# Encoder layer with dilated attention on one core: scores and value products both on 64x64 tiles of the array

## The chip, the core and the metric

The kernel runs on one NeuronCore of a Trainium2 chip. Its engines have names in the profile: PE is TensorE (matmuls; PEld are its weight loads), DVE is VectorE, ACT is ScalarE, POOL is GpSimd, and SP issues most DMAs. The metric is the device time of one execution in microseconds (us), as the median of several runs. A lower number is better.

## What is computed

Two independent sequences (1024 tokens, width 1024, float32) pass through one encoder layer. Cut to what matters here:

```python
h = rmsnorm(x, norm_mix)
z = h @ w_in                                   # pool channels, then q, k, v of 12 heads of 64
a = pool_mixer(z[..., :512], pool_maps, pool_scale) @ w_up_pool
b = attention_branch(z[..., 512:]) @ w_up_attn
gates = sigmoid(h @ w_gate + b_gate)
x = x + (g_a * a + g_b * b) @ w_out
h = rmsnorm(x, norm_ffn)
x = x + (silu(h @ w_ffn_gate) * (h @ w_ffn_up)) @ w_ffn_down
return rmsnorm(x, norm_final)
```

`attention_branch` has three groups of four heads with dilations 1, 4 and 16. Each query sees the keys of a window around it (`softmax(q k^T / 8) v`), and the three groups are merged by a softmax over their log-sum-exp values. `pool_mixer` takes window means of four channel groups and multiplies each group with a 128x128 map.

## The kernel before

**The large products.** All large matrix products are done in three float32r matmuls each (high x high, low x high, high x low part, lines 1080 to 1082) and by a seven-product scheme: "product m" (`pair_product`) is twelve matmuls over 512 columns on the full 128x128 array. In the front part there are 133 such products per sequence (`FRONT`), and their sums go through banks 0 to 3 of PSUM, which has eight banks.

**The attention** is woven into these products by a fixed schedule. A *unit* is 128 queries of one pair of heads, a *duo* is two units, and there are 24 duos per sequence: duos 0 to 7 are group 0 (a query tile sees up to 256 keys that lie in two tiles of values, so the value products of its two units are separate), 8 to 15 group 1 (both units of a duo share their keys), 16 to 23 group 2 (128 keys each). From product `ATT0` on, duo `d` takes these steps:

- `scores(d)`: per unit and head h one plain float32 matmul, with the 64 rows of the head as contraction and 128 queries as columns, thus on a 64x128 tile of the array, into bank 4+h. The profile shows two records for one such matmul, one for each of its two passes.
- `softmax_duo(d)` on DVE (two mask additions in PSUM at line 1968, maximum, negation), and `exp_duo(d)` on ACT.
- `prob_transposes(d)` on PE, ahead of an even-numbered step's product, into banks 6 (first unit) and 7 (second unit), and `evict_probs(d)` on ACT, which copies them to `probT`.
- `prob_v(d)` on PE, ahead of the next product: per value tile and head one float32 matmul with 128 rows (64 where only half a tile of keys lies at an edge of the sequence) and the head's 64 value columns, thus on a 128x64 tile, accumulating in bank 6. Behind it stand at once `scores(d + 2)`, and then the product.
- `evict_duo(d)` on ACT (line 1564) copies bank 6 to `o_st` and signals `o_ready`; a DMA stores it. The next `prob_transposes` waits for `o_ready` before it writes bank 6.

So per sequence PE has 22 places where value products are followed directly by scores, two where value products stand alone (the last two duos) and two where scores do (the first two).

**The pool mixer** runs between these. For each of eight jobs e per sequence DVE forms window sums (line 1992) and means (2002), ACT rounds them, DVE takes the low part `pool_lo` (2008), and PE multiplies (`mix_channels`, three matmuls into **bank 7**) directly behind the product of step `ATT0 + 10 + 6e`. ACT reads bank 7 in `evict_mix` (line 1582), which stands in ACT's order behind the rounding of the operand of a later product (`operand_hi`, line 1488), and signals `mix_read`. For e = 0 to 6 the next thing in PE's order is a `prob_v`; that makes 14 such places in the two sequences.

Every engine works through its own list in order. A PE instruction that has a wait holds everything behind it on PE. `bank_read(b)` makes PE wait for the last reader of bank b.

Of the kernel before, what the change touches and what calls it, by code (L numbers as in the profile page):

```python
# [156 lines left out]
def slot_of(m):  # L157
# [9 lines left out]
    "p1_copied": N_PAIRS, "sums_done": 5 * N_PAIRS,  # L167
    "rope_read": 24, "qk_ready": 24, "c11_copied": N_VP + N_SPILL, "vt_full": 12, "vst_ready": 12,
    "s_full": N_DUOS, "masked": 2 * N_DUOS, "negmax_ready": N_DUOS, "p_ready": N_DUOS, "pt_full": N_DUOS,
    "pt_ready": N_DUOS, "o_full": N_DUOS, "o_ready": N_DUOS,  # L170
    "pooled_ready": 8, "pool_hi_ready": 8, "pool_ready": 8, "mix_full": 8, "mix_read": 8, "mix_hi_ready": 4,
    "mixed_ready": 4, "diff_ready": 1, "weight_ready": 1, "coef_ready": 1, "coef_hi": 1, "coef_split": 1, "sel_ready": 1, "cT_zero": 1, "cT_full": 1, "cT_ready": 1,
    "ct_full": 12, "ct_read": 12, "two_merged": 4, "merged": 2,
# [25 lines left out]
def due(name, s, n):  # L199

    step = 16 if name in DMA_SEMS else 1
    return (s * PER_SEQ[name] + n) * step
# [43 lines left out]
def encoder(nc, x, w_in, maps, w_up_pool, w_up_attn, w_gate, w_out, w_fg, w_fu, w_fd,  # L246
# [3 lines left out]
    with ctx:  # L250
# [102 lines left out]
        def small(name, shape):  # L353
# [16 lines left out]
        sems = {name: sem(name) for name in PER_SEQ}  # L370
        (ssx_ready, stdx_ready, ss_ready, std_ready, xn_ready, mix_made, tr_full, shi_ready, s_ready, t_made, thi_ready, t_ready, prod_done,
         p1_copied, sums_done, rope_read, qk_ready, vt_full, vst_ready, s_full, masked,
         negmax_ready, p_ready, pt_full, pt_ready, o_full, o_ready, pooled_ready, pool_hi_ready, pool_ready, mix_full,
         mix_read, mix_hi_ready, mixed_ready, diff_ready, weight_ready, coef_ready, coef_hi, coef_split, sel_ready, cT_zero, cT_full,
         cT_ready, ct_full, ct_read, two_merged, merged, mhi_ready,
         mT_ready, wu_hi_ready, wu_ready, up_full, sig_ready, a_read, b_read, y_sum, yhi_ready, y_ready, wo_hi_ready,
# [691 lines left out]
        def _(pe):  # L1068
# [35 lines left out]
            def scores(s, duo):  # L1104

                for unit in (2 * duo, 2 * duo + 1):
                    g, p, b = unit // UNITS, unit // TT, unit % TT
                    lo, wid, _, _ = window(g, b)
                    if b == 0:
                        pe.wait_ge(qa_in[p % 2], due(f"qa_in{p % 2}", s, p // 2 + 1))  # L1110
                    if unit == 0:
                        pe.wait_ge(qk_ready, due("qk_ready", s, 24))
                    c = 256 * (unit % 2)
                    for h in range(2):
                        if unit % 2 == 0:
                            bank_read(4 + h)
                        rows = slice(HEAD * h, HEAD * h + HEAD)
                        ins = nc.tensor.matmul(ps[:, 4 + h, c:c + wid], qk[p % 2][rows, 0, b * P:(b + 1) * P],
                                               qk[p % 2][rows, 1, lo:lo + wid], start=True, stop=True)
                ins.then_inc(s_full, 1)  # L1120
                for h in range(2):
                    last[4 + h] = ("p_ready", s, duo + 1)
# [16 lines left out]
            def prob_v(s, duo):  # L1139

                pe.wait_ge(pt_ready, due("pt_ready", s, duo + 1))
                bank_read(6)
                g, p = 2 * duo // UNITS, 2 * duo // TT
                if duo % 4 == 0:
                    pe.wait_ge(va_in[p % 2], due(f"va_in{p % 2}", s, VA_DUE[p]))

                for us in ((slice(0, 2),) if g == 1 else (slice(0, 1), slice(1, 2))):
                    tiles = window(g, (2 * duo + us.start) % TT)[2]
                    for c, v in enumerate(tiles):
                        length = v_tokens(g)[v][1]  # L1150
                        for h in range(2):
                            rows = slice(HEAD * h, HEAD * h + HEAD)
                            ins = nc.tensor.matmul(ps[rows, 6, us.start * P:us.stop * P], V[p % 2][0:length, v, rows],
                                                   probT[0:length, us, h * len(tiles) + c, :], start=(c == 0),
                                                   stop=(c == len(tiles) - 1), skip_group_check=True)
                ins.then_inc(o_full, 1)
                last[6] = ("o_ready", s, duo + 1)

            def value_transposes(s, g, c):

# [249 lines left out]
        def _(act):  # L1410
# [149 lines left out]
            def evict_duo(s, duo):  # L1560

                act.wait_ge(o_full, due("o_full", s, duo + 1))
                act.wait_ge(o_stored[duo % 2], due(f"o_stored{duo % 2}", s, duo // 2))
                nc.scalar.copy(o_st[:, duo % 2, :], ps[:, 6, 0:2 * P]).then_inc(o_ready, 1)

            def round_maps(s):

# [276 lines left out]
        def _(dve):  # L1844
# [113 lines left out]
            def softmax_duo(s, duo):  # L1958
# [14 lines left out]
                else:  # L1973
                    for u, (_, wid, _, _) in enumerate(kinds):
# [3 lines left out]
                V_.tensor_scalar(st[:, p % 2, qb:qb + 2, 0:2].rearrange("p u h -> p h u"), mx[:, :, :],  # L1978
                                 -HEAD ** -0.5, None, ALU.mult).then_inc(negmax_ready, 1)

            def window_sums(s, e, ks):


                g, h = POOL_JOBS[e]
                if ks[0] == 0:
                    dve.wait_ge(uh_in, due("uh_in", s, e + 1))
                    pad = slice(0, 8) if h == 0 else slice(H2 + 8, H2 + 16)
                    chain.link(V_.memset(Uh[:, pad], 0.0))
                sums = [Uh, pw1, pw0, pw1, pw0]
                for k in ks[:max(g + 1 - ks[0], 0)]:  # L1990
                    n = H2 + 16 - (2 << k) + 1
                    chain.link(V_.tensor_tensor(sums[k + 1][:, 0:n], sums[k][:, 0:n], sums[k][:, (1 << k):n + (1 << k)],
                                                ALU.add))
# [188 lines left out]
            for s in range(SEQS):  # L2182
# [12 lines left out]
                for m in range(FRONT + 1):  # L2195
# [9 lines left out]
                        final_norm(s - 1, 1 + m)  # L2205
                    if m == ATT0 - 2:
                        softmax_duo(s, 0)
                    if 0 <= duo < N_DUOS - 1 and step == 1:
                        softmax_duo(s, duo + 1)
                    e, stage = pool_step(m)  # L2210
# [146 lines left out]
```

## Time and profile before

| | before |
|---|---|
| time, median of 3 runs (range) | 2582.65 us (2581.26 to 2584.28) |
| span of the profiled execution | 2579.1 us |
| median less this span | 3.55 us |
| PE busy | 2529.2 us, 98% |
| DVE, ACT, POOL busy | 50%, 41%, 67% |

The span is the time from the first to the last instruction of the one execution that was profiled; the time of a run has some microseconds more, before and behind its instructions. That profiled execution's own time is not recorded, so the runs' median stands beside its span. PE's busy share counts a matmul as busy until its modelled end, so start-to-start distances tell more than busy time does.

### The profile page before, as it was taken

The numbers are of one execution on the slowest core, as the hardware profiler recorded it, in microseconds if no ns is written. First come the engines' busy times: TensorE is split into PE (matmuls) and PEld (weight loads), VectorE is DVE, ScalarE is ACT, GpSimd is POOL, SyncE is SP. The second block draws the span as 40 slices with busy tenths as digits, with TensorE's granted clock in tenths as the row PEclk, the third lists the DMA queues.
The fourth block names the chain that finished last, engine by engine and source line by source line (L and its number), as shares of the span: only waits on it lengthen the run. The fifth ranks groups of instructions, "written<-read, shape, count | busy, mean of one in ns | idle before, by whom it ended". The sixth has DMA issues, their size and how long they took to land. (4 is left out here: it accounts for less than half of the span.)

```text
span 2579.1 us, 33371 instructions
## 1 busy us (share of the span) xinstructions
PE 2529.2 (98%) x12048; PEld 2067.6 (80%) x12048; DVE 1296.0 (50%) x1761; ACT 1051.4 (41%) x2034; POOL 1736.9 (67%) x1288
## 2 busy tenths in 40 slices
PE   6999999999999999999999999999999999999998
PEld 5887777888788888888778877778878888888887
DVE  6753557654422222378878445556443222223858
ACT  5224554444433333345542345544443333333445
POOL 7775455645888888757567654564468888887543
PEclk8999999999999999999999999999999999999999
DMA  4444555462233333374453535554623333334634
GB/s 137 125 132 127 146 155 168 160 239 81 86 100 109 102 107 99 131 232 153 135 162 99 159 107 153 161 169 164 232 82 95 98 96 113 99 110 152 198 123 145
DMA packets 331859, 350.76 MB, mean 136 GB/s; under 512 B 30641, under 2 KB 242993, under 8 KB 330161
## 3 DMA queue, kind: packets, MB, share of 16 engines
q1 hardware_dynamic: 329968, 344.32, 42.4%
q10 hardware_dynamic: 1728, 4.30, 0.5%
q8 instruction: 98, 1.61, 0.3%
q14 instruction: 65, 0.52, 0.1%
HBM read 249.28 MB, written 99.29 MB: 135 GB/s over the span
## 5 line engine op out<-in xcount | busy, mean ns | idle before, releaser
L1080 PE MATMUL ps<-S,t_hi 128*128 128x512 f32 (+2 forms) x2336 | 917.0, 393 | 8.9 <-POOL t_lo L856 6.3
L1082 PE MATMUL ps<-S,t_lo 128*128 128x512 f32 (+2 forms) x2336 | 903.7, 387 | 0.0
L1081 PE MATMUL ps<-S,t_hi 128*128 128x512 f32 (+2 forms) x2336 | 903.0, 387 | 0.0
L1080 PEld LDWEIGHTS ps<-S,t_hi 128*128 128x128 f32 x2336 | 438.6, 188 | 110.6 <-issue 12.3
L1082 PEld LDWEIGHTS ps<-S,t_lo 128*128 128x128 f32 x2336 | 438.6, 188 | 89.6
L1081 PEld LDWEIGHTS ps<-S,t_hi 128*128 128x128 f32 x2336 | 439.1, 188 | 83.9
L856 POOL TENSOR_TENSOR t_lo<-wraw,t_hi 128x512 fp32r<-128x512 f32 x185 | 246.0, 1330 | 205.0 <-ACT t_hi L1488 202.7
L856 POOL TENSOR_TENSOR t_lo<-wraw_ff,t_hi 128x512 fp32r<-128x512 f32 x225 | 293.8, 1307 | 89.9 <-ACT t_hi L1488 84.9
L856 POOL TENSOR_TENSOR t_lo<-R,t_hi 128x512 fp32r<-128x512 f32 x154 | 219.9, 1432 | 181.4 <-ACT t_hi L1488 181.4
L1488 ACT CAST t_hi<-wraw_ff 128x512 fp32r<-128x512 f32 x225 | 139.6, 623 | 366.7 <-PE ps L1082 366.5
L1080 PE MATMUL ps<-t_hi,d_hi 128*128 128x512 f32 x616 | 241.4, 392 | 1.1 <-POOL t_lo L856 1.1
L1082 PE MATMUL ps<-t_hi,d_lo 128*128 128x512 f32 x616 | 240.2, 390 | 0.0
L1081 PE MATMUL ps<-t_lo,d_hi 128*128 128x512 f32 x616 | 240.2, 390 | 0.0
L1488 ACT CAST t_hi<-wraw 128x512 fp32r<-128x512 f32 x185 | 115.2, 624 | 303.7 <-PE ps L1082 298.3
L2133 DVE TENSOR_TENSOR d_lo<-d_raw,d_hi 128x512 fp32r<-128x512 f32 x154 | 135.8, 884 | 105.7 <-ACT d_hi L1679 105.3
L1916 DVE TENSOR_TENSOR u<-u,ps 128x512 f32<-128x512 f32 x82 | 56.3, 687 | 256.5 <-PE ps L1082 256.5
L1679 ACT CAST d_hi<-d_raw 128x512 fp32r<-128x512 f32 x154 | 95.5, 620 | 194.8 <-PE ps L1082 161.9
L856 POOL TENSOR_TENSOR t_lo<-t,t_hi 128x512 fp32r<-128x512 f32 x74 | 102.0, 1379 | 98.0 <-ACT t_hi L1488 97.7
L1919 DVE TENSOR_TENSOR v<-u,ps 128x512 f32<-128x512 f32 x82 | 56.3, 687 | 195.5 <-PE ps L1082 195.4
L987 POOL TENSOR_TENSOR wo_lo<-wo_raw,wo_hi 128x1024 fp32r<-128x1024 f32 x32 | 81.2, 2541 | 89.2 <-ACT wo_hi L1645 89.2
L1080 PEld LDWEIGHTS ps<-t_hi,d_hi 128*128 128x128 f32 x616 | 116.1, 188 | 26.1 <-POOL t_lo L856 2.5
L856 POOL TENSOR_TENSOR t_lo<-t_ff,t_hi 128x512 fp32r<-128x512 f32 x90 | 116.0, 1289 | 29.6 <-ACT t_hi L1488 29.6
(170 smaller groups left out, 4027.4 us busy)
## 6 DMA issues: line engine op xcount, KB each, us to landing
d_raw<-d_rows SPq DMA_DIRECT2D x154, 256.0 KB, 3.1
d_rows<-act_f SPq DMA_DIRECT2D x110, 256.0 KB, 2.1
wraw_ff<-w_ffn_up SPq DMA_DIRECT2D x44, 512.0 KB, 4.6
R<-w_ffn_down SPq DMA_DIRECT2D x88, 256.0 KB, 3.1
wraw<-w_in SPq DMA_DIRECT2D x42, 512.0 KB, 5.9
sp_rows<-gst SPq DMA_DIRECT2D x80, 256.0 KB, 2.5
wraw_ff<-w_ffn_gate SPq DMA_DIRECT2D x40, 512.0 KB, 4.8
wo_raw<-w_out SPq DMA_DIRECT2D x36, 512.0 KB, 3.3
```

Source lines behind the costliest of these rows:

```text
L856: nc.gpsimd.tensor_tensor(shape(t_lo[r][:, :]), src, shape(t_hi[r][:, :]).bitcast(F32), ALU.subtract).then_inc(t_ready, 1)
L987: nc.gpsimd.tensor_tensor(wo_lo[r][:, :], wo_raw[op % 2][:, :], wo_hi[r][:, :].bitcast(F32), ALU.subtract).then_inc(wo_ready, 1)
L1080: nc.tensor.matmul(o_ps, w[0], r[0], start=begins, stop=False, skip_group_check=True)
L1081: nc.tensor.matmul(o_ps, w[0], r[1], start=False, stop=False, skip_group_check=True)
L1082: return nc.tensor.matmul(o_ps, w[1], r[0], start=False, stop=ends, skip_group_check=True)
L1488: nc.scalar.copy(dst, src).then_inc(thi_ready, 1)
L1679: nc.scalar.copy(d_hi[d % 4][:, :], d_raw[d % 4][:, :]).then_inc(dhi_ready, 1)
L1916: V_.tensor_tensor(u, u, b1, ALU.add).then_inc(sums_done, 1)
L1919: V_.tensor_tensor(v1[:, :], u, b2, ALU.add).then_inc(sums_done, 1)
L2133: V_.tensor_tensor(d_lo[d % 4][:, :], d_raw[d % 4][:, :], d_hi[d % 4][:, :].bitcast(F32), ALU.subtract).then_inc(d_ready, 1)
```

## The change

The change touches only the attention's two kinds of matmuls, and what reads the second kind.

- `scores`: each matmul over 128 queries becomes two over 64 queries each, into partitions 0 to 63 and 64 to 127 of the same bank. The tiles are 64x64.
- `prob_v`: each matmul over 128 keys becomes two over 64 keys each. Keys 0 to 63 of every value tile accumulate in bank 6, keys 64 to 127 in bank 7. The tiles are 64x64. Where a tile has just 64 keys there is no second one. PE waits for the last reader of bank 7 as well.
- `evict_duo` copies bank 6 to `o_st` and signals `o_half` in place of `o_ready`. A new DVE step, `sum_duo`, adds bank 7 to `o_st` and signals `o_ready`. It stands ahead of the duo's `softmax_duo` in DVE's order.

```diff
@@ scores
-                        ins = nc.tensor.matmul(ps[:, 4 + h, c:c + wid], qk[p % 2][rows, 0, b * P:(b + 1) * P],
-                                               qk[p % 2][rows, 1, lo:lo + wid], start=True, stop=True)
+                        for r in range(2):
+                            at_q = b * P + HEAD * r
+                            ins = nc.tensor.matmul(ps[HEAD * r:HEAD * r + HEAD, 4 + h, c:c + wid],
+                                                   qk[p % 2][rows, 0, at_q:at_q + HEAD],
+                                                   qk[p % 2][rows, 1, lo:lo + wid], start=True, stop=True)
@@ prob_v
                 bank_read(6)
+                bank_read(7)
...
-                    for c, v in enumerate(tiles):
-                        length = v_tokens(g)[v][1]
-                        for h in range(2):
-                            rows = slice(HEAD * h, HEAD * h + HEAD)
-                            ins = nc.tensor.matmul(ps[rows, 6, us.start * P:us.stop * P], V[p % 2][0:length, v, rows],
-                                                   probT[0:length, us, h * len(tiles) + c, :], start=(c == 0),
-                                                   stop=(c == len(tiles) - 1), skip_group_check=True)
+                    keys = [[(c, v) for c, v in enumerate(tiles) if v_tokens(g)[v][1] > HEAD * r] for r in range(2)]
+                    for n in range(len(tiles)):
+                        for r in range(2):
+                            if n >= len(keys[r]):
+                                continue
+                            c, v = keys[r][n]
+                            some = slice(HEAD * r, HEAD * r + HEAD)
+                            for h in range(2):
+                                rows = slice(HEAD * h, HEAD * h + HEAD)
+                                ins = nc.tensor.matmul(ps[rows, 6 + r, us.start * P:us.stop * P], V[p % 2][some, v, rows],
+                                                       probT[some, us, h * len(tiles) + c, :], start=(n == 0),
+                                                       stop=(n == len(keys[r]) - 1), skip_group_check=True)
                 ins.then_inc(o_full, 1)
-                last[6] = ("o_ready", s, duo + 1)
+                last[6] = last[7] = ("o_ready", s, duo + 1)
@@ evict_duo (ACT)
-                nc.scalar.copy(o_st[:, duo % 2, :], ps[:, 6, 0:2 * P]).then_inc(o_ready, 1)
+                nc.scalar.copy(o_st[:, duo % 2, :], ps[:, 6, 0:2 * P]).then_inc(o_half, 1)
@@ new on DVE
+            def sum_duo(s, duo):
+
+                dve.wait_ge(o_half, due("o_half", s, duo + 1))
+                o = o_st[:, duo % 2, :]
+                V_.tensor_tensor(o, o, ps[:, 7, 0:2 * P], ALU.add).then_inc(o_ready, 1)
@@ DVE's order in the front part
+                    if 1 <= duo <= N_DUOS and step == 1:
+                        sum_duo(s, duo - 1)
                     if 0 <= duo < N_DUOS - 1 and step == 1:
                         softmax_duo(s, duo + 1)
```

On PE, behind the pool product of the first job, stood this (line numbers of before; `64x128` is output partitions by columns):

```order
L1080 MATMUL ps<-pool_hi,maps_hi 128x512 [waits pt_ready,mixed_maps,pool_ready]
L1081 MATMUL ps<-pool_lo,maps_hi 128x512
L1082 MATMUL ps<-pool_hi,maps_lo 128x512
L1153 MATMUL ps<-probT,V_att_116 64x128 [waits va_in1,pt_ready]
L1153 MATMUL ps<-probT,V_att_116 64x128 x7
L1118 MATMUL ps<-qk_att_114 128x256 [waits p_ready] x2
L1118 MATMUL ps<-qk_att_114 128x256 x2
L1080 MATMUL ps<-S,t_hi_83 128x512 [waits sums_done,t_ready]
```

At the same place there stands now (the value products are line 1162, the scores line 1120):

```order
L1080 MATMUL ps<-pool_hi,maps_hi 128x512 [waits pt_ready,mixed_maps,pool_ready]
L1081 MATMUL ps<-pool_lo,maps_hi 128x512
L1082 MATMUL ps<-pool_hi,maps_lo 128x512
L1162 MATMUL ps<-probT,V_att_116 64x128 [waits mix_read,va_in1,pt_ready]
L1162 MATMUL ps<-probT,V_att_116 64x128 x13
L1120 MATMUL ps<-qk_att_114 64x256 [waits p_ready]
L1120 MATMUL ps<-qk_att_114 64x256
L1120 MATMUL ps<-qk_att_114 64x256 [waits p_ready]
L1120 MATMUL ps<-qk_att_114 64x256 x5
L1080 MATMUL ps<-S,t_hi_83 128x512 [waits sums_done,t_ready]
```

The value products are 14 in place of 8 (16 where no edge of the sequence is touched), the scores 8 in place of 4, and the first value product now waits for `mix_read` too.

On DVE, in the stretch of the seventh pool job (four window sums), the end of the pool work and the following softmax stood like this:

```order
L2002 SCALAR_TENSOR_TENSOR Uh<-pw_123,Uh 128x512 [waits dve_chain]
L1922 TENSOR_TENSOR gst_121<-v_97,ps 128x512 [waits gst_stored1,sums_done,prod_done]
L1968 TENSOR_TENSOR ps<-ps,diag_sb 128x2x128 [waits s_full]
L1968 TENSOR_TENSOR ps<-ps,diag_sb 128x2x128
L1972 TENSOR_REDUCE mx<-ps 128x4 [waits masked]
L1978 TENSOR_SCALAR st<-mx 128x2x2 [waits st_stored1,dve_chain]
L1924 TENSOR_TENSOR gst_120<-u_0_95,ps 128x512 [waits gst_stored0,prod_done]
L2008 TENSOR_TENSOR pool_lo<-Uh,pool_hi 128x512 [waits pool_hi_ready]
```

And there stands now (line 1994 is the new step):

```order
L2017 SCALAR_TENSOR_TENSOR Uh<-pw_123,Uh 128x512 [waits dve_chain]
L1931 TENSOR_TENSOR gst_121<-v_97,ps 128x512 [waits gst_stored1,sums_done,prod_done]
L1994 TENSOR_TENSOR o_st<-o_st,ps 128x256 [waits o_half]
L1977 TENSOR_TENSOR ps<-ps,diag_sb 128x2x128 [waits s_full]
L1977 TENSOR_TENSOR ps<-ps,diag_sb 128x2x128
L1981 TENSOR_REDUCE mx<-ps 128x4 [waits masked]
L1987 TENSOR_SCALAR st<-mx 128x2x2 [waits st_stored1,dve_chain]
L1933 TENSOR_TENSOR gst_120<-u_0_95,ps 128x512 [waits gst_stored0,prod_done]
L2023 TENSOR_TENSOR pool_lo<-Uh,pool_hi 128x512 [waits pool_hi_ready]
```

The new addition is behind the pool sums and ahead of the masks; nothing else changed its place. SP's list is the same as before.

## Rows read from the trace of the kernel before

**Rows 1.** The page, busy time per engine and granted PE clock in 40 slices

```profile
PE 2529.2 (98%) x12048; PEld 2067.6 (80%) x12048; DVE 1296.0 (50%) x1761; ACT 1051.4 (41%) x2034; POOL 1736.9 (67%) x1288
...
PEclk8999999999999999999999999999999999999999
```

**Rows 2.** Waits of PE, 200 to 620 and 1480 to 1900: total, times, longest

```profile
PE ps L1080 <- DVE pool_lo L2008: 0.9, 2, 0.8
...
PE ps L1080 <- DVE pool_lo L2008: 0.8, 1, 0.8
```

**Rows 3.** Timeline of PE around one duo of group 1: start, duration, matmuls

```profile
307.04 0.39 PE L1082 MATMUL ps<-S,t_lo 128*128 128x512 f32 x1
307.36 0.44 PE L1153 MATMUL ps<-probT,V_att 128*64 128x256 f32 x2
307.62 0.82 PE L1153 MATMUL ps<-probT,V_att 128*64 128x256 f32 x6
308.06 0.39 PE L1153 MATMUL ps<-probT,V_att 128*64 128x256 f32 x2
308.37 0.49 PE L1118 MATMUL ps<-qk_att 64*128 64x256 f32 x2
308.69 0.60 PE L1118 MATMUL ps<-qk_att 64*128 64x256 f32 x4
309.12 0.38 PE L1118 MATMUL ps<-qk_att 64*128 64x256 f32 x2
309.44 0.50 PE L1080 MATMUL ps<-S,t_hi 128*128 128x512 f32 x1
309.77 0.39 PE L1081 MATMUL ps<-S,t_hi 128*128 128x512 f32 x1
```

**Rows 4.** Timeline of PE, value products of three duos of group 0

```profile
236.13 1.39 PE L1153 MATMUL ps<-probT,V_att 128*64 128x128 f32 x16
...
245.10 1.09 PE L1153 MATMUL ps<-probT,V_att 128*64 128x128 f32 x16
...
262.18 1.24 PE L1153 MATMUL ps<-probT,V_att 128*64 128x128 f32 x16
```

**Rows 5.** Timeline behind two pool products, and all evictions (line 1582)

```profile
271.68 1.39 PE L1153 MATMUL ps<-probT,V_att 128*64 128x128 f32 x16
271.79 0.69 ACT L1582 ACTIVATE Uh<-ps,p_scale 128x512 f32<-128x512 f32 x1
...
325.19 0.66 ACT L1488 CAST t_hi<-wraw 128x512 fp32r<-128x512 f32 x1
325.34 1.08 PE L1153 MATMUL ps<-probT,V_att 128*64 128x256 f32 x8
325.71 0.73 ACT L1582 ACTIVATE Uh<-ps,p_scale 128x512 f32<-128x512 f32 x1
...
L1582 ACT ACTIVATE Uh<-ps,p_scale x16: 682/687/727, 271.8 to 1726.0; 128x512 f32<-128x512 f32 x16
```

**Rows 6.** Timeline: a duo's eviction, the following softmax, and the next transposes

```profile
326.47 0.37 ACT L1564 COPY o_st<-ps 128x256 f32<-128x256 f32 x1
...
327.54 0.70 DVE L1968 TENSOR_TENSOR ps<-ps,masks_sb 128x512 f32<-128x512 f32 x1 [2.10 <-PE ps L1118]
...
330.28 0.82 PE L1133 MATMUL ps<-ident_sb,prob 128*128 128x128 f32 x6
```

**Rows 7.** Groups by form (256-column mask), then the timeline in the seventh pool job

```profile
L1968 DVE TENSOR_TENSOR ps<-ps,diag_sb 128x256 f32<-128x256 f32 x16 | 6.1, 427 | 8.9 <-PE ps L1118 8.9
...
419.62 0.60 PE L1133 MATMUL ps<-ident_sb,prob 128*128 128x128 f32 x4
...
419.92 0.76 DVE L1968 TENSOR_TENSOR ps<-ps,diag_sb 128x256 f32<-128x256 f32 x2
...
422.49 1.38 DVE L2008 TENSOR_TENSOR pool_lo<-Uh,pool_hi 128x512 fp32r<-128x512 f32 x1
...
423.93 0.50 PE L1080 MATMUL ps<-pool_hi,maps_hi 128*128 128x512 f32 x1 [0.79 <-DVE pool_lo L2008]
```

More of the change, by code:

```diff
@@ L169 @@
     "s_full": N_DUOS, "masked": 2 * N_DUOS, "negmax_ready": N_DUOS, "p_ready": N_DUOS, "pt_full": N_DUOS,
-    "pt_ready": N_DUOS, "o_full": N_DUOS, "o_ready": N_DUOS,
+    "pt_ready": N_DUOS, "o_full": N_DUOS, "o_half": N_DUOS, "o_ready": N_DUOS,
     "pooled_ready": 8, "pool_hi_ready": 8, "pool_ready": 8, "mix_full": 8, "mix_read": 8, "mix_hi_ready": 4,
@@ L372, in encoder @@
          p1_copied, sums_done, rope_read, qk_ready, vt_full, vst_ready, s_full, masked,
-         negmax_ready, p_ready, pt_full, pt_ready, o_full, o_ready, pooled_ready, pool_hi_ready, pool_ready, mix_full,
+         negmax_ready, p_ready, pt_full, pt_ready, o_full, o_half, o_ready, pooled_ready, pool_hi_ready, pool_ready, mix_full,
          mix_read, mix_hi_ready, mixed_ready, diff_ready, weight_ready, coef_ready, coef_hi, coef_split, sel_ready, cT_zero, cT_full,
```

## The prediction

> **What bounds the kernel now.** I read the page first: PE is busy 98% of the span, the others 67% or less, and the granted clock is full (2.4 GHz) but for the ends [rows 1]. Next the waits of PE in the two stretches with attention: PE waits there for another engine for 1.7 us in all, three times, each time for `pool_lo` from DVE [rows 2]. So the attention parts are set by PE's own stream, and whatever shortens or lengthens that stream moves the end by as much. Then the timeline of PE around one duo, start by start [rows 3]. The reader is to see there that two heads' records start together (two records last 0.44 us where one lasts 0.43), that steps inside a kind of tile are 0.215 us apart (256 columns, one of two passes), and that each change of the tile's shape costs twice: the last step before it takes about 0.1 longer, since the array runs empty, and the first step behind it takes longer by the weight load that nothing covers. 307.04 to 307.36 is 0.32 where these full-array matmuls follow one another every 0.23. 307.36 to 307.62 is 0.26 in place of 0.215. 308.06 to 308.37 is 0.31, 308.37 to 308.69 is 0.32, 309.12 to 309.44 is 0.32, and the first product step 0.33 in place of 0.23.
>
> **What the change removes.** Value products and scores then have one shape, so the switch between them goes: 308.06 to 308.37 becomes a plain step (0.31 - 0.215 = 0.095), and the first scores' weights load behind the last value product (0.32 - 0.215 = 0.105) [rows 3]. That is 0.20 us at each of 22 places in each of two sequences, 8.8 us. The switches into and out of the pair stay.
>
> At the edges of the sequence a 64-key value tile made a 64x64 tile among 128x64 ones. These value products last 1.39 or 1.24 us where others last 1.09 [rows 4], so 0.30 and 0.15 more. Four duos of each kind (two per sequence, one for each head pair of group 0) give 4 x 0.30 + 4 x 0.15 = 1.8 us. Where scores stand alone (four places), the uncovered weight load has 64 columns in place of 128: 0.045 in place of 0.105, 0.2 us in all.
>
> **What it adds on PE.** Twice as many matmuls, each on a quarter of the array. Per duo the array holds as much work as before if four tiles run side by side: before, two tiles of half the array did. That columns run side by side is seen in value products, that rows do in scores [rows 3]; four at once are not in this trace. The bound from below is nothing. From above, if only two run side by side, all steps of both kinds double. I take nothing, because each of the two directions is shown at full rate. The records of a group start some 0.007 us apart, so the last of four starts about 0.015 later, which the drain at the end pays once for each of 48 duos: 0.7 us.
>
> The sum of gains is 8.8 + 1.8 + 0.2 - 0.7 = 10.1 us.
>
> **What it adds as a wait.** Value products now write bank 7, and 14 of them stand directly behind a pool product, which writes bank 7 too. They must wait for `evict_mix` to read it. Before, the value products started at 271.68, and that eviction ended at 271.79 + 0.69 = 272.48: 0.80 later. In the other kind, ACT is still rounding an operand (325.19, 0.66) when the pool product ends, so the eviction ends at 325.71 + 0.73 = 326.44 against 325.34: 1.10 [rows 5]. Ten of the 14 places are like the first, four like the second (0.98 to 1.10), together 12.2 us. ACT's order and its distance to PE's stream are the same as before, so the ends of the evictions stay where they are. What is queued behind the waiting value products is the scores and the next product, everything PE has; nothing covers it. A wait that ended for PE at 422.49 + 1.38 = 423.87 let its matmul start at 423.93 [rows 7], so 0.06 x 14 = 0.8 us more. 13.0 us.
>
> **What it adds on DVE.** 48 additions of 256 columns with one operand in PSUM. The nearest row is the mask over 256 columns, 427 ns alone and 0.34 to the next behind it (two in 0.76) [rows 7]. For most duos it lies in a hole: `o_st` is copied by 326.84, DVE had been idle 2.10 us when it began the masks at 327.54, and the sum takes until about 327.3. It is ready 3 us ahead of the transposes at 330.28, which now need it for both banks [rows 6]. In the narrower group 2 it pushes the masks back by some 0.1 us, with three products of time before the transposes need them.
>
> It lies open where DVE is late already. In the seventh pool job of each sequence DVE reaches the masks at 419.92, over 3 us behind the scores. The transposes start at 419.62 and would have to wait until the sum, 419.95 + 0.43, so 0.8 us or a little more. But PE then waited at the following pool product anyway until 423.93 for `pool_lo` [rows 7], so this wait only moves forward; what counts is how much later `pool_lo` comes: 0.35 for the sum and 0.09 for the one before it, and the 0.2 that PE saves in this stretch is lost in the wait. I take 0.6 us for each of the two sequences, and 0.1 for the third place where PE waited for `pool_lo`: 1.3 us. Bounds: nothing (if the new stops of PE let DVE catch up) and 2 x 1.1 + 0.4 = 2.6 (if the waits add up).
>
> **The sum** is 13.0 + 1.3 - 10.1 = +4.2 us against the profiled span: 2583.3. With the 3.55 us between that span and the runs' median it is **2586.8 us**, 0.16% above 2582.65. About 0.2% (5.2 us) is what a measurement of this kernel tells from no change, so this counts as no change, near its upper border of 2587.8. The parts leave a spread of some 4 us: DVE's bounds above (-1.3, +1.3), weight loads of the scores that still show (+1 to +4.6 if none is covered: 44 x 0.105), a stop that costs 0.1 less or more (1.4 either way).
>
> **The rivals.**
>
> *Only two tiles run side by side.* For it: no row has four plain float32 tiles at once. Against it: both directions are seen, and in rows of 64 keys two tiles ran in the 64x64 shape. Price: each duo's steps double, 8 steps of 0.215 in groups 0 and 1 (1.7 us for 32 duos), half of it for 16: 55 + 14 = 69 us, so 2656.
>
> *PE's instruction stream becomes the bound.* A duo of group 0 then has 32 + 16 records in place of 16 + 8. Before, 16 records took 1.09 us [rows 4], 0.068 each with the last one's own length in it, so this is an upper bound for the price of one. At 0.068, the 48 records take 3.3 us where the array needs 1.7; the 32 records of a duo take 2.2 where it needs 1.7 in group 1 and 0.9 in group 2. 16 x 1.6 + 16 x 0.5 + 16 x 1.3 = 54 us, so 2641. Against it: two records follow each other within 0.01 us [rows 3], which speaks for a queue that is filled ahead.
> The Trainium skill, "TensorE: Matmul & The Clock Gate", section "Wait — 56ns, not 53.3ns?", states about 62 ns per MATMUL where the sequencer decodes in software, and a floor of about 25 ns otherwise. By 62 ns the same sum gives 42 us and some 2629; by 25 ns nothing is lost. The bound of 68 ns leaves both open, and the distance of 0.01 us inside a pair leans to the second.
>
> *The stops of PE are hidden (faster side).* If the stops let late work catch up, `pool_lo` (1.7 us of waits, and the 1.3 above) is there in time: 2586.8 - 3.0 = 2583.8, still no change. To get below 2577.5 the switches into and out of the pair (0.1 for running empty and 0.1 for weights at the way out, 0.1 and 0.045 at the way in [rows 3]) must get cheaper too, since the tiles are smaller. It decides from 0.13 us per duo on; at 0.2 it gives 2583.8 - 9.6 = 2574. For it: a 64-column load is shorter. Against it: the matmuls behind the way out have full weights as before, and the way in loads 64 columns now as well.
>
> *The addition on DVE delays each duo.* Against it are the 3 us of slack [rows 6]. If it did, the price would be 0.4 in 48 places, 19 us, so 2606.
>
> **Chances.** The sum as worked out 0.75 (2583 to 2591: I give 0.50 to its part below 2587.8 and 0.25 to that above); two tiles only 0.07; instruction stream 0.06; DVE delay in many duos 0.03; hidden stops without cheaper switches 0.02, which is again no change; cheaper switches 0.07. So faster by over 0.2% is 0.07, within 0.2% 0.52, slower by over 0.2% 0.41. The range must leave out no more than 0.2: from 2579 to 2600 it holds the first case, the hidden stops, and weak forms of the instruction stream and of the DVE case.
>
> **What the changed profile would show.** Value products and scores back to back in one shape, with steps of 0.215 across the border, four records starting within 0.03. PE waiting 14 times ahead of value products for the eviction of bank 7, 0.8 to 1.1 us each. PE waiting for `o_st` from DVE ahead of the transposes in the seventh pool job of each sequence, and nowhere else over 0.1 us. DVE's sums at 0.43 us each. The prediction is wrong if records of one duo take much over 0.215 per step (two tiles only, or the stream), if the stops are much shorter than 0.8, or if the first step of the scores still shows its weight load.

## The result, and the profile after

| | before | after |
|---|---|---|
| median (range) | 2582.65 us (2581.26 to 2590.49) | 2588.18 us (2586.33 to 2590.88) |
| ratio | | 1.0019, 95% interval 1.0011 to 1.0027 |
| span of the profiled execution | 2579.1 us | 2584.9 us |

The changed kernel takes 4.9 us more by the ratio (2.8 to 7.0). It was predicted to take 4.2 us more. That lies just under what I had called the limit of a measurement here (5.2 us), and this comparison, with 11 runs of each kernel, puts it above zero.

The page of the changed kernel, busy time and PE's granted clock, against [rows 1]:

```profile
PE 2520.0 (97%) x12912; PEld 2065.1 (80%) x12912; DVE 1312.8 (51%) x1809; ACT 1052.8 (41%) x2034; POOL 1736.4 (67%) x1288
...
PEclk8999999999999999999999999999999999999999
```

PE has 864 more matmuls and is busy for 9 us less, yet the span is longer: the time went into waits. The waits of PE in the two stretches with attention (200 to 640 and 1480 to 1900; total, times, longest), against [rows 2]:

```profile
PE ps L1162 <- ACT Uh L1591: 6.8, 7, 1.1
PE ps L1136 <- DVE o_st L1994: 1.1, 1, 1.1
...
PE ps L1080 <- DVE pool_lo L2023: 0.2, 1, 0.2
...
PE ps L1162 <- ACT Uh L1591: 6.9, 7, 1.2
PE ps L1136 <- DVE o_st L1994: 1.1, 1, 1.1
```

Line 1162 holds the value products, 1591 is the eviction of bank 7, 1136 the transposes, 1994 the new addition. The same duo of group 1 as in [rows 3], on PE's timeline:

```profile
306.45 0.39 PE L1082 MATMUL ps<-S,t_lo 128*128 128x512 f32 x1
306.77 0.45 PE L1162 MATMUL ps<-probT,V_att 64*64 64x256 f32 x4
...
307.25 0.61 PE L1162 MATMUL ps<-probT,V_att 64*64 64x256 f32 x8
...
307.47 0.40 PE L1162 MATMUL ps<-probT,V_att 64*64 64x256 f32 x4
...
307.68 0.40 PE L1120 MATMUL ps<-qk_att 64*64 64x256 f32 x4
...
307.90 0.83 PE L1120 MATMUL ps<-qk_att 64*64 64x256 f32 x12
...
308.65 0.51 PE L1080 MATMUL ps<-S,t_hi 128*128 128x512 f32 x1
```

(A row starts with its first record, and answers for different windows cut the records differently; only the starts matter.) Four records start together, and four together still last 0.40. The step is 0.215, and it stays 0.215 across the border from value products to scores (307.47 to 307.68 to 307.90), where it had been 0.31 and 0.32. From the first value product to the next big product it is 1.88 in place of 2.08. The steps into and out of the pair, 0.32 each, are as before. A duo of group 0, whose value products have 128 columns each, shows how fast the records can follow one another:

```profile
244.46 1.10 PE L1162 MATMUL ps<-probT,V_att 64*64 64x128 f32 x32
245.38 0.94 PE L1120 MATMUL ps<-qk_att 64*64 64x256 f32 x16
```

The first score record starts 0.92 behind the first of 32 value records, 0.029 for each.

Two stops (places behind a pool product where PE now stands still until ACT has read bank 7), on PE and ACT, against [rows 5]:

```profile
270.01 0.40 PE L1082 MATMUL ps<-pool_hi,maps_lo 128*128 128x512 f32 x1
271.39 0.45 PE L1162 MATMUL ps<-probT,V_att 64*64 64x128 f32 x8 [0.98 <-ACT Uh L1591]
...
270.45 0.69 ACT L1591 ACTIVATE Uh<-ps,p_scale 128x512 f32<-128x512 f32 x1
...
324.19 0.40 PE L1082 MATMUL ps<-pool_hi,maps_lo 128*128 128x512 f32 x1
325.72 0.45 PE L1162 MATMUL ps<-probT,V_att 64*64 64x256 f32 x4 [1.14 <-ACT Uh L1591]
...
324.33 0.66 ACT L1497 CAST t_hi<-wraw 128x512 fp32r<-128x512 f32 x1
324.85 0.73 ACT L1591 ACTIVATE Uh<-ps,p_scale 128x512 f32<-128x512 f32 x1
```

The eviction ends at 271.14 and at 325.58. PE starts 0.25 and 0.14 later, where I had put 0.06.

The addition (all 48, by line; ns), then PE's and DVE's timelines in the seventh pool job, against [rows 7]:

```profile
L1994 DVE TENSOR_TENSOR o_st<-o_st,ps x48: 412/421/423, 237.6 to 1717.8; 128x256 f32<-128x256 f32 x48
```

```profile
420.79 0.39 PE L1082 MATMUL ps<-S,t_lo 128*128 128x512 f32 x1
...
421.70 0.41 DVE L1994 TENSOR_TENSOR o_st<-o_st,ps 128x256 f32<-128x256 f32 x1
...
422.26 0.63 PE L1136 MATMUL ps<-ident_sb,prob 128*128 128x128 f32 x4 [1.08 <-DVE o_st L1994]
...
424.27 1.38 DVE L2023 TENSOR_TENSOR pool_lo<-Uh,pool_hi 128x512 fp32r<-128x512 f32 x1
```

**Where the 5.8 us between the two spans are.** I paired the same matmuls of the two traces and took the differences of the distances between their starts, summed over all places:

| part | predicted | traces |
|---|---|---|
| attention matmuls, first record to next product (52 blocks) | -10.1 | -10.5 |
| 14 stops behind pool products | +13.0 | +14.6 |
| transposes that wait for the addition (+2.5), less the shorter waits for `pool_lo` (-1.5) | +1.3 | +1.0 |
| sum | +4.2 | +5.1 |

The remaining 0.7 us lie outside the change. The largest pieces are +1.2 at 648 (a wait for `wo_lo` of 2.6 us, 1.4 before) and -1.6 between 1298 and 1302, where the trace of before has PE's clock at half for 3.4 us and the trace of after does not. Whether these go with the kernel or with the execution, one trace of each can't tell.

### The profile page after: what moved, and what is told of

It is laid out like the page before. It is cut to its first block and busy times, and to the rows that moved or that the text cites. A ratio compares the mean times of both kernels' runs of the same rounds, so it can differ in the third digit from the quotient of the medians.

```text
span 2584.9 us, 35159 instructions
## 1 busy us (share of the span) xinstructions
PE 2520.0 (97%) x12912; PEld 2065.1 (80%) x12912; DVE 1312.8 (51%) x1809; ACT 1052.8 (41%) x2034; POOL 1736.4 (67%) x1288
```

## The experiments

Beside each run stands the median of the kernel before on the same chip (one chip for e1 to e4, one for e5 to e8, one for e9 and e10). The ratio, and not the median, is what compares runs of different chips. "Later" or "behind" before, in us, is said of a trace where the same matmul of a large product starts that much later than in the trace of before.

| run | median us | before | ratio (95% interval) |
|---|---|---|---|
| e1_scores_only | 2584.19 | 2582.56 | 1.0006 (0.9997 to 1.0015) |
| e2_values_only | 2595.43 | 2582.56 | 1.0048 (1.0035 to 1.0061) |
| e3_wait_only | 2597.84 | 2582.56 | 1.0060 (1.0047 to 1.0072) |
| e4_sum_only | 2583.33 | 2582.56 | 1.0003 (0.9994 to 1.0012) |
| e5_mix_late | 2577.66 | 2583.37 | 0.9981 (0.9972 to 0.9989) |
| e6_mix_mid | 2584.84 | 2583.37 | 1.0005 (0.9996 to 1.0014) |
| e7_before_late | 2590.32 | 2583.37 | 1.0026 (1.0016 to 1.0036) |
| e8_late_order | 2575.68 | 2583.37 | 0.9968 (0.9956 to 0.9980) |
| e9_wait_carried | 2586.64 | 2581.55 | 1.0019 (1.0010 to 1.0029) |
| e10_late_order2 | 2573.09 | 2581.55 | 0.9968 (0.9958 to 0.9978) |

My theory: the change saves some 10 us of tile switches and edge tiles, which only the common shape brings, and pays some 14 us of stops for bank 7. The rivals: the small tiles are faster by themselves, or the added instructions or the addition cost the time, or the stops are free.

### e1: the scores alone on 64x64 tiles

```diff
-                        ins = nc.tensor.matmul(ps[:, 4 + h, c:c + wid], qk[p % 2][rows, 0, b * P:(b + 1) * P],
...
+                        for r in range(2):
+                            at_q = b * P + HEAD * r
+                            ins = nc.tensor.matmul(ps[HEAD * r:HEAD * r + HEAD, 4 + h, c:c + wid],
+                                                   qk[p % 2][rows, 0, at_q:at_q + HEAD],
...
```

> Kernel before, with the scores alone on 64x64 tiles; value products stay on 128x64 tiles in one bank, so no wait for bank 7 and no addition on VectorE. Theory A (the gain of the change comes from the border between value products and scores, which costs 0.1 us for the array running empty and 0.1 for a weight load that nothing covers): the border is still there, only the first load has 64 columns in place of 128 (0.045 in place of 0.105), 48 x 0.06 = 2.9 us less at the most, so 2580 to 2582.6, ratio 0.999 to 1.000. Rival B (the scores themselves run faster as four small tiles, whatever stands next to them): most of the 10.5 us that the attention blocks lost is here, so 2573 to 2575, ratio 0.9965. Rival C (twice the matmuls cost time in the instruction stream): above 2583.

The time is within the noise: 1.0006, which is above theory A's upper end of 1.000 but whose interval holds it. The trace is sharper. The attention blocks shrink by 2.7 us in all, 0.04 to 0.05 in each ordinary one (four edge duos 0.20), where the full change gave 0.19 to 0.20. So rival B falls. Rival C (above 2583) names the time that was measured, but not its cause: the blocks shrink, so 384 more matmuls cost nothing there.

The four edge duos are a test of their own. Their last value tile has 64 keys, so it was a 64x64 tile before too, and in e1 the scores behind it have the same shape:

```profile
264.93 0.43 PE L1120 MATMUL ps<-qk_att 64*64 64x256 f32 x2
265.06 0.28 PE L1156 MATMUL ps<-probT,V_att 64*64 64x128 f32 x2
```

The first scores start ahead of the last value records, and the border is gone: 0.16 more than in an ordinary duo, from the common shape alone.

That the profiled span is 3.4 us longer comes from elsewhere. This execution is 2.0 us behind ahead of any attention, 1.6 of them between 40 and 42, where PE's clock is still at half (0.58 from 38 to 45, 0.98 in the trace of before). And PE once waits 2.5 us for `v` from DVE at 441, with half clock for 3.4 us behind it; e7 below has the same wait.

### e2: the value products alone on 64x64 tiles

The edit is that of the change without its scores part.

> Kernel after, with the scores back on 64x128 tiles; value products on 64x64 tiles in banks 6 and 7, with the addition on VectorE. Theory A: the border to the scores is still a change of shape, so only the mixed tiles at the sequence's edges are saved (-1.8); the 14 stops behind pool products stay (+14.6 by the trace of after) and so does the late addition in the seventh pool job (+1.0): 2582.65 + 13.8 = 2596.5, ratio 1.0053. With e1 the two parts alone then sum to about +11, where both together gave +5: the difference, 6 to 9 us, is what the common shape saves. Rival B (value products on four tiles save time by themselves): under 2592.

1.0048 is +12.4 us (+13.8 expected, inside the interval). The blocks shrink by 1.4 us, all of it in the eight edge duos (4 x 0.30 and 4 x 0.15); in every other duo the small tiles cost 0.01. The stops are 14.8 us. e1 and e2 together saved 2.7 + 1.4 = 4.1 us in the blocks, the change 10.5. The 6.4 between are the common shape: 0.16 in each of 40 duos. In the other four, the edge duos above, e1 alone already had it. (By time, the two halves cost 1.6 and 12.4, 14.0 us together, where about 11 was expected and the whole change costs 4.9.)

### e3: only the wait

```diff
                 bank_read(6)
+                bank_read(7)
```

> Kernel before, with nothing but one more wait of TensorE: ahead of each duo's value products it waits until ScalarE has read bank 7 (mix_read), though the value products still write bank 6 alone. Theory A (what the change costs is this wait, in 14 places behind a pool product): +14.6 us by the gaps in the trace of after, so 2597, ratio 1.0055; by the price that the prediction used, 0.06 us between the end of the eviction and the first matmul, +13.0, so 2595.7. The gaps will show 0.14 us between the end of the eviction and the first value product where one wait stands there, about 0.25 where the wait for the stored v stands there too. Rival D (the stop lets late work of other engines catch up, so that part of it comes back): under 2592. Rival E (the wait costs little, and the time of the change goes to other things, as the added matmuls): 2583.

1.0060, or +15.5 us (12.1 to 18.6). With not one matmul changed, this line costs all that the stops cost: the gaps sum to +14.8 us. Ten of the matmuls start 0.144 to 0.146 behind the eviction's end, four 0.255 to 0.257. Nothing came back (rivals D and E fall). At the last of the 14, a wait of 0.80 for `pool_lo` ended at 1719.1 and the stop of 0.87 at 1720.9. PE's clock went to half behind them, from 1721.0 for 3.4 us, and that cost another 1.6.

### e4: only the addition's place

```diff
-                nc.scalar.copy(o_st[:, duo % 2, :], ps[:, 6, 0:2 * P]).then_inc(o_ready, 1)
+                nc.scalar.copy(o_st[:, duo % 2, :], ps[:, 6, 0:2 * P]).then_inc(o_half, 1)
...
+                V_.tensor_tensor(o, o, ps[:, 6, 0:2 * P], ALU.max).then_inc(o_ready, 1)
```

> Kernel before, with nothing but one more step on VectorE for each duo: behind the copy of o_st it takes the maximum of o_st and bank 6 (256 columns, one operand in PSUM), which leaves the values as they are, and the transposes wait for it. Theory A (it lies in VectorE's holes but for the seventh pool job of each sequence): +1.0 us, at most +2.6, so 2583.5 to 2585.3, ratio 1.0004 to 1.001. Rival F (each duo is delayed by it): 48 x 0.4 = +19, so 2602. Rival G (nothing at all, since the wait for pool_lo shrinks by as much): 2582.65, ratio 1.0000.

1.0003 (+0.8 us; the interval holds both theory A and rival G). Rival F falls. PE's waits in the two stretches show why it is nearly nothing:

```profile
PE ps L1133 <- DVE o_st L1985: 0.7, 1, 0.7
...
PE ps L1133 <- DVE o_st L1985: 0.7, 1, 0.7
```

The wait for the addition is there (the gaps ahead of two transposes grow by 0.86 each, 1.7 in all), and the waits for `pool_lo` [rows 2] are gone (-1.7). Here rival G is right: the wait only moved forward. In the changed kernel it costs 1.0. That PE comes to the transposes earlier there, by what the common shape has saved, fits the other traces: the wait is 0.7 in e2 and e4, which lack that gain, and 1.1 in the changed kernel, e5, e6 and e9, which have it.

### e9: the same waits in another order

```diff
+                bank_read(7)
                 pe.wait_ge(pt_ready, due("pt_ready", s, duo + 1))
                 bank_read(6)
-                bank_read(7)
```

> Kernel after, with the same waits ahead of the value products in another order: the one for bank 7 (mix_read) is written first and the one for the transposed probabilities (pt_ready) behind it. In the trace of after, the first-written wait rides on the first weight load, and the others stand ahead of it as semaphore instructions of their own; the wait for bank 7 was one of these, and the value products start 0.144 us after the eviction's end, and 0.25 where a further semaphore instruction follows. Theory A (this is the mis-sized term of the prediction): with the wait on the weight load itself, all 14 starts come 0.05 to 0.07 us after the eviction's end, -0.9 -0.8 = -1.7 us in the attention, 2586.5, which the medians can barely tell, but the gaps can. Rival L (the longer start comes from the change of the tile's shape or the smaller tiles, not from the semaphore instructions): gaps stay at 0.144 and 0.25, 2588.2.

The same two stops:

```profile
270.43 0.69 ACT L1591 ACTIVATE Uh<-ps,p_scale 128x512 f32<-128x512 f32 x1
271.17 0.98 PE L1162 MATMUL ps<-probT,V_att 64*64 64x128 f32 x26 [0.78 <-ACT Uh L1591]
271.94 0.38 PE L1120 MATMUL ps<-qk_att 64*64 64x256 f32 x2
271.98 0.28 PE L1162 MATMUL ps<-probT,V_att 64*64 64x128 f32 x2
...
324.58 0.73 ACT L1591 ACTIVATE Uh<-ps,p_scale 128x512 f32<-128x512 f32 x1
325.36 0.88 PE L1162 MATMUL ps<-probT,V_att 64*64 64x256 f32 x12 [1.05 <-ACT Uh L1591]
```

All 14 matmuls start 0.052 or 0.053 behind the eviction's end, and the stops sum to 12.8 us in place of 14.6. That is the prediction's 13.0, so its size was missed by the semaphore instruction that stood between the wait and the matmul: about 0.09 for one and 0.2 for two. In the medians 1.8 us is not to be seen (ratio 1.0019 again). Rival L falls.
The Trainium skill, "Perfetto Trace Analysis", section "Identifying Dependency Chains", says that an instruction that waits for several engines may have semaphore instructions put ahead of it. The trace agrees: in the changed kernel such instructions of 0.051 us start at 271.17 and 271.28, between the eviction's end and the first weight load at 271.36; in e9 none stands there.

### e5 and e6: the pool product moved

(Shortened. `inner` is a new argument of the product; the calls at the old places go.)

```diff
                 for k in range(4):
                     ins = three(...)
+                    if k == 0 and inner:      # e6: k == 1
+                        inner()               # mix_channels; e5: one product later, e6: in the product that it followed
...
+                    if pool_step(m)[1] == 4:  # e5, on ScalarE, behind evict_duo; e6: stage 3, ahead of the next operand
+                        evict_mix(s, pool_step(m)[0])
```

> Kernel after, with each pool product moved one operand product on: it stands behind the first of the four k blocks of the next big product, behind the value products and the scores, and ScalarE evicts it there. By then VectorE has read bank 7, and the eviction (0.9 + 0.7 us) ends before the transposes need the bank. Theory A (the 14 stops behind pool products are all that the change costs beyond 1 to 2 us): the stops of 0.9 to 1.2 us ahead of value products go, -14.6, and the waits for pool_lo with them (-0.2), so 2588.2 - 14.8 = 2573.4, ratio to before 0.9964. The o_st waits in the seventh pool job stay, 1.2 each. Rival H (the transfers of Uh, which start 4 to 6 us later now, come too late for VectorE, whose lateness goes on to the transposes): up to 3.5 us at one or two jobs of each sequence, 2576 to 2582. Rival I (the stops let late work elsewhere catch up, and other waits take their place): above 2582.

0.9981: 9.8 us less than the changed kernel, and below the kernel before. Theory A gave 14.8. In the two stretches with attention the paired starts drift by -3.2 and -2.9 us against before, where the changed kernel drifted by +2.8 and +3.0, so 11.9 of the expected 14.8 are there. What is missing there stands in part in waits for DVE that grew. In the first stretch:

```profile
PE ps L1080 <- DVE v L1927: 1.0, 2, 0.8
PE ps L1080 <- DVE o_st L1993: 0.3, 1, 0.3
```

The wait for `v` was 0.4 in the changed kernel (in e5, 0.8 of the 1.0 lie behind the attention, where before has 0.7 too), and no product or pool product (line 1080 holds both) waited for `o_st`. The rest of it is spread over gaps of 0.3 and less, which I did not take apart. Another part of the gain was lost outside these stretches, in this one execution: 1.9 us ahead of the first attention (1.2 of them with the clock at half from 40 on, as in e1), and the clock at 647 (last section). So rival I holds for some 3 us and falls for the rest. Rival H names the time that was measured (2576 to 2582); how much of the 3 us is due to later transfers of Uh was not taken apart.

> Kernel after, with each pool product moved forward by half a product: behind the second of the four k blocks of the product that it follows in kernel after, and ScalarE evicts it ahead of the next operand's rounding. The eviction then lies beside the other half of that product. Theory A: the stops go too (-14.6), but in the sixth and seventh job, where pool_lo comes 0.06 us ahead of the pool product in kernel after, and in the eighth (0.8), the pool product now waits for it up to 1.4 us in the middle of the product, four to five places, +5: 2588.2 - 14.6 + 5 = 2578.6, ratio 0.9985. If pool_lo were no limit, 2573.5, as with the later placement.

1.0005, 3.6 us less than the changed kernel and 5 to 6 more than expected. The mechanism is as forecast, the sizes are not: PE's waits for `pool_lo` rose to 6.7 us, three of up to 1.5 in each sequence, and a stop of 0.6 is left in each:

```profile
PE ps L1080 <- DVE pool_lo L2022: 3.4, 3, 1.5
...
PE ps L1162 <- ACT Uh L1591: 0.6, 1, 0.6
```

### e7: the later pool product in the kernel before

> Kernel before, with the pool products moved as in the later placement (behind the first k block of the next big product). Theory A: kernel before has no stop behind pool products, so the placement gives only the waits for pool_lo (1.7 us): 2581, ratio 0.9993; the gain of the later placement in kernel after is the stop. Rival J (the placement itself is worth as much, for example by fewer changes of the tiles' shape between the products): 2570 to 2575. Rival H (late transfers of Uh): 2583 to 2588.

1.0026, slower by 6.7 us. The placement alone is worth nothing in a kernel without the stops, so rival J falls. Theory A is wrong about its cost: it had -1.7. Rival H comes near the size (at most 2588) and has part of the mechanism. Once in each sequence, in the eighth pool job, PE waits for `v` from DVE, 2.5 and 2.8 us. DVE, POOL and PE of this run there:

```profile
437.81 1.14 DVE L2000 TENSOR_TENSOR pw<-pw,edge_sb 128x8 f32<-128x8 f32 x1
438.99 1.71 DVE L2001 SCALAR_TENSOR_TENSOR Uh<-pw,Uh 128x512 f32<-128x512 f32 x1
440.62 0.67 DVE L1918 TENSOR_TENSOR v<-u,ps 128x512 f32<-128x512 f32 x1
...
437.31 1.63 POOL L902 TENSOR_TENSOR t<-wraw,t 128x512 f32<-128x512 f32 x1
...
441.44 0.76 PE L1080 MATMUL ps<-S,t_hi 128*128 128x512 f32 x1 [2.51 <-DVE v L1918]
```

The same steps of DVE in the kernel before:

```profile
437.84 1.14 DVE L2001 TENSOR_TENSOR pw<-pw,edge_sb 128x8 f32<-128x8 f32 x1
439.01 0.69 DVE L2002 SCALAR_TENSOR_TENSOR Uh<-pw,Uh 128x512 f32<-128x512 f32 x1
```

And PE's windows in e7 (length, busy, count, granted clock, then the DMA engines' busy share and GB/s):

```profile
438.50:441.40 2.90, 0.43 (x2) 1.00 0.72 151
441.40:443.00 1.60, 1.56 (x4) 0.51 0.32 129
443.00:444.50 1.50, 1.50 (x5) 0.50 0.42 160
444.50:446.00 1.50, 1.50 (x7) 0.88 0.00 0
```

`v` stands behind the window sums and means on DVE. DVE was late with them in both places. In the first sequence, DVE began this work at 432.66, 1.05 us earlier than before (433.71), but PE was 1.73 ahead, so DVE was 0.7 behind by PE's measure. Then three of the window sums took 4.28 us in place of 3.25, and the means 1.71 in place of 0.69. In the second sequence the transfer of Uh came 3.47 us later than before, with PE 2.10 later, and the sums took 4.11 in place of 2.17; the means took 1.71, and 1.74 in the kernel before too. So rival H's late transfers are a part of it (0.7 and 1.4 us), and the longer steps of DVE are the rest.

DVE's steps stretch there while POOL works beside them. The 8-column step took 1.14 here and in the kernel before, where it ended within 0.03 us of the end of a step of POOL (here at 438.95 and 438.94), and 0.17 in the seventh job of the changed kernel (420.30), with POOL idle. That POOL is the cause was not tested. Nor does it need the moved pool product: e1, where nothing of the pool mixer was touched, has the first of the two waits as well. So e7 shows that the placement brings no gain by itself, and not that it always costs 6.7 us.

The wait had a price behind it too: the clock stood at half for 3.4 us. With it, each of the two places cost 4.3 and 4.7 us against before.

### e8 and e10: VectorE's order, and one block later

(Shortened; the last window sum and the means go from their old place.)

```diff
                         sum_duo(s, duo - 1)
...
+                    if stage == 2 and POOL_JOBS[e][0] == 3:
+                        window_sums(s, e, (3,))
+                        window_means(s, e)
```

> The kernel with the later pool products, and on VectorE, in the jobs with the widest pooling windows, the last window sum and the means stand behind the addition of the value products' halves in place of ahead of it. Theory A: the addition is then there in time in the seventh pool job, the two waits of TensorE for o_st (1.2 us each) go: 2573.4 - 2.4 = 2571.0, ratio to before 0.9955. Rival K (what is moved back makes pool_lo or the masks late in its place): no difference or up to +2 to the kernel without this edit.

0.9968, the median 2.0 us below that of e5; the intervals overlap, so that e8 is faster than e5 is not shown by the times. The two waits of the transposes are gone (their gaps are back to before's). New ones stand behind them (0.9 for o_st ahead of the pool product, 0.7 for gst in the eighth job, in each sequence). So theory A's step is there and rival K takes much of it back.

> The kernel with later pool products and VectorE's other order, with two more edits: the pool product stands behind the second k block in place of the first (0.69 us later), and the waits ahead of value products in the order of the run above. Theory A: the waits of the pool products for o_st (0.9, once in each sequence) shrink by up to 0.7 each, -1.4 us, so 2574.3 and a ratio to before of 0.996. Rival K (VectorE's lateness in the last three pool jobs decides, and another wait takes its place): 2575.7, no difference.

0.9968, the same ratio as e8. The times can't tell theory A from rival K here, which lie 1.4 us apart. By the trace, the waits for o_st shrank from 0.9 to 0.2 and 0.3 as expected, and others grew (gst to 1.5 in one sequence, v to 1.4 in the other): rival K. These two are the fastest versions, 8.3 us below the kernel before (5.7 to 10.8 for e10).

## Why the prediction was right

Its account held in all but one term: a gain of 10 us, stops of 13 (they came to 14.6, see below), a small cost on DVE, a sum of a few us on the slow side.

- **The border.** 0.20 saved less 0.015 of skew was forecast for each of 44 duos; the traces show 0.19 to 0.20. By e1, 0.04 of it is the shorter weight load of the scores alone; by e1 and e2, 0.16 is the common shape, which needs both sides of the border to have it. The weight load behind the border is fully covered, so the spread that I kept for it was not needed. The switches into and out of the pair did not get cheaper (0.32 each, as before), so the rival on the faster side falls.
- **The edges** gave 1.8 us, as forecast, and e2 shows it apart (4 x 0.30 and 4 x 0.15).
- **Scores alone** saved 0.04 in each of four places, 0.16 us, with 0.2 forecast.
- **Four tiles** do run side by side, and the instruction stream is no bound: in group 1, 16 records take 0.91 us from the first value product to the first score, four of them starting within 0.02, and in group 0, 32 records take 0.92. The rivals "two tiles" and "instruction stream" are out. The price of 62 ns for a MATMUL, from the page of the Trainium skill that the prediction cites, would make 1.98 us of these 32, so it does not apply here.
- **The stops** are 14, as forecast. Ten follow the first pattern and four the second, and the evictions end where they ended before against PE. The step that was mis-sized is the release, "0.06 x 14 = 0.8 us". I took 0.06 from a wait that a weight load carries itself [rows 7]. The new wait stood in a semaphore instruction of its own ahead of the load, so it is 0.144, and in four places 0.25 with another such instruction behind it. That makes 2.5 us in place of 0.8, which e9 takes back to 0.7. e3 shows that the wait alone bears the whole cost.
- **The addition** was hidden where I said, took 0.42 (0.43), and showed only in the seventh job. Its waits are 1.2 longer gaps at two places, with 1.5 us less for `pool_lo`: +1.0 where I had 1.3. e4 shows that without PE's own gain it nets to nothing.
- **Two misreadings without effect.** The view behind [rows 2] also has a wait for `v` in each stretch, 0.7 and 0.5 us, where I wrote that PE waits for nothing but `pool_lo`. Both lie behind the attention (at 450 to 620 and behind 1725) and are 0.4 and 0.5 in the changed kernel, so the sum does not move. And the clock of the kernel before is not full everywhere between the ends: it stands at half for 3.4 us at 1298, and [rows 1], with slices of 64 us, does not show that.

The errors in part went against each other (the stops 1.6 too low, the gain 0.4 too low, DVE 0.3 too high), so the sum came nearer to the measured time than its worst term, which is luck. What I did not foresee, and what only e5 to e10 showed, is how much of a gain PE can keep: of the 15 us that the stops cost, their removal brought back 12 in the stretches with attention and 10 in the time.

## What to carry to other kernels

A tile shape shared by neighbours on TensorE is worth its switch (here 0.16 us at each border, and 0.04 for the smaller weights), and one side alone does not bring it unless its neighbour already has the shape. Before spreading an accumulation over a second bank, list who else uses that bank and who stands directly behind them: one wait, in 14 places, cost more than 44 cheaper borders gave, and moving the other user by part of a product turned +4.9 us into -4.9. When pricing a wait, look whether the instruction carries it or another instruction stands between, and write the wait that ends last first.

## What was unexpected on the hardware

**Tiles run independently across the border.** In e9, two score records start at 271.94 and two records of value products, written earlier in the program, at 271.98. So one tile is at the scores while another is still at the value products. It shows where the tiles have unequal amounts of work: in seven of the eight edge duos of the changed kernel, in the four of e1 above, and in no other duo of the two.

**The same wait can cost the clock or not.** In the changed kernel and in e5, PE waits 2.60 us for `wo_lo` at the same place of the program. PE's windows (length, busy, count, clock, DMA share, GB/s), first of the changed kernel:

```profile
649.00:651.60 2.60, 0.04 (x1) 1.00 0.42 125
651.60:653.20 1.60, 1.56 (x7) 1.00 0.19 45
```

and of e5:

```profile
645.00:647.60 2.60, 0.02 (x1) 0.96 0.38 113
647.60:649.20 1.60, 1.60 (x4) 0.50 0.18 49
649.20:650.80 1.60, 1.60 (x7) 0.50 0.93 279
650.80:653.00 2.20, 2.20 (x14) 1.00 0.00 0
```

The changed kernel stays at full clock (2.4 GHz), e5 runs at half (1.2 GHz) for some 3 us, which costs half of them. The trace of e1 has the same wait and is like the changed kernel, that of e8 is like e5. The length of the wait alone does not decide it; what does stays open. The 14 stops of 0.9 to 1.2 us did not bring the changed kernel's clock down: it is 1.00 in both stretches with attention. In e3 the clock did fall once, behind the last of the same stops, which had another wait of 0.80 just ahead of it.
